# Out-projection of a hybrid decoder layer: token tiles 1 to 6 formed in three pairs, by seven half products a pair instead of eight

## What is computed

```
y = jnp.concatenate([ya, yb, yc, yd.astype(x.dtype)], axis=-1) @ w_out[l]
x = x + gt1 * y
h2 = rms_norm(x, norm2_g[l]) * (1.0 + sc2) + sh2
x = x + gt2 * hier_moe(h2, moe_w_grp[l], moe_b_grp[l], moe_w_exp[l], moe_b_exp[l],
                       moe_w_gate[l], moe_w_up[l], moe_w_down[l])
```

## Time and profile before

| | |
|---|---|
| time, median of 3 runs | 858.77 us (858.05 to 859.92) |
| the profiled execution, its own time | 855.52 us |
| its span | 853.8 us |
| TensorE busy | 800.3 us, 94% of the span |
| VectorE busy | 467.6 us, 55% |
| chain that ended last | TensorE 76%, VectorE 13%, issue 3%, DMA 3% |
| mean granted TensorE clock | 0.983 of full |
| moved by DMA | 136.30 MB, mean 160 GB/s |

### The profile page before, as it was taken

One profiled execution on the slowest core, in us unless ns is written; L12 is line 12 of the kernel. 1 busy time (PEld: TensorE's weight loads), 2 busy tenths in 40 slices (PEclk: granted clock), 3 DMA queues, 4 the chain that ended last, 5 costly groups with the idle time before them and its releaser, 6 DMA issues.

```text
span 853.8 us, 16617 instructions
## 1 busy us (share of the span) xinstructions
PE 800.3 (94%) x6791; PEld 534.1 (63%) x6791; DVE 467.6 (55%) x1174; ACT 236.2 (28%) x565; POOL 283.7 (33%) x267
## 2 busy tenths in 40 slices
PE   8999999999999999798989999999899999999950
PEld 8557544454444444787776555555888888888830
DVE  3850468888742134889873344354745555554534
ACT  6320021111200031466542122212232223232214
POOL 5820000000299800744660000000235656543332
PEclk9999999999999999999999999999999999999995
DMA  9934433344201020300003851213889999988639
GB/s 319 334 94 136 148 123 124 123 149 157 90 25 50 25 74 16 136 4 4 5 5 147 317 203 50 87 63 123 323 316 302 305 273 278 275 266 261 209 66 385
DMA packets 79716, 136.30 MB, mean 160 GB/s; under 512 B 17213, under 2 KB 51226, under 8 KB 79642
## 3 DMA queue, kind: packets, MB, share of 16 engines
q1 hardware_dynamic: 69338, 118.44, 39.9%
q0 software_dynamic: 10304, 16.82, 8.4%
HBM read 124.18 MB, written 29.92 MB: 180 GB/s over the span
## 4 chain that ended last, share of the span: by engine, by line
PE 76%; DVE 13%; issue 3%; DMA 3%; ACT 2%; POOL 1%; SPq 1%; DVEq 0%; POOLq 0%; ACTq 0%
PE banks L791 71%; PE banks L1430 3%; DVE REG_Y L1790 3%; DVE REG_P L2392 1%; DVE REG_P L2041 1%; POOL REG_P L677 1%; PE banks L1361 1%; ACT REG_P L1478 1%; DMA REG_P<-y_d 1%; ACT REG_W L1478 1%; DMA prow<-in_conv_w 1%; DVE REG_W L1897 1%; DVE REG_P L1790 1%; DVE mx L1900 1%; DMA y_d<-REG_Y,idx 1%
## 5 line engine op out<-in xcount | busy, mean ns | idle before, releaser
L791 PE MATMUL banks<-REG_W 128*128 128x512 f32 (+2 forms) x832 | 273.0, 497 | 0.3 <-DVE REG_W L1830 0.3
L791 PEld LDWEIGHTS banks<-REG_W 128*128 128x128 f32 (+1 forms) x832 | 125.6, 182 | 133.1 <-issue 132.3
L791 PE MATMUL banks<-REG_W,REG_Y 128*128 128x512 f32 x256 | 118.3, 600 | 1.4 <-DVE REG_Y L2347 1.1
L1478 ACT ACTIVATE REG_P<-banks 128x256 f32<-128x256 f32 (+2 forms) x102 | 46.4, 480 | 144.8 <-PE banks L791 126.4
L791 PE MATMUL banks<-REG_P 64*64 64x64 f32 (+3 forms) x2496 | 72.4, 236 | 11.3 <-issue 4.5
L791 PEld LDWEIGHTS banks<-REG_P 64*64 64x64 f32 (+1 forms) x2496 | 62.4, 138 | 20.4 <-issue 9.1
L1478 ACT ACTIVATE REG_Y<-banks,mod,s 128x128 f32<-128x128 f32 x136 | 51.1, 456 | 86.0 <-PE banks L1430 86.0
L791 PEld LDWEIGHTS banks<-REG_W,REG_Y 128*128 128x128 f32 x256 | 45.6, 191 | 44.3 <-issue 44.1
L791 PEld LDWEIGHTS banks<-REG_Y,REG_P 128*128 128x128 f32 (+1 forms) x616 | 63.1, 181 | 6.7 <-issue 6.7
L791 PE MATMUL banks<-REG_Y,REG_P 128*128 128x128 f32 (+1 forms) x616 | 66.5, 276 | 0.0
L635 POOL TENSOR_TENSOR REG_P<-REG_P 128x1040 f32<-128x1040 f32 x2 | 4.8, 2386 | 175.8 <-DVE REG_P L1876 175.8
(11 more groups left out here) (297 smaller groups left out, 1107.7 us busy)
## 6 DMA issues: line engine op xcount, KB each, us to landing
REG_P<-in_w_ada SPq DMA_DIRECT2D x20, 1024.0 KB, 6.7
REG_W<-in_w_in SPq DMA_DIRECT2D x17, 512.0 KB
REG_P<-in_moe_w_gate SPq DMA_DIRECT2D x17, 512.0 KB, 8.5
REG_W<-in_moe_w_gate SPq DMA_DIRECT2D x16, 512.0 KB, 5.7
REG_W<-in_moe_w_up SPq DMA_DIRECT2D x16, 512.0 KB, 10.1
REG_W<-in_moe_w_down SPq DMA_DIRECT2D x16, 512.0 KB, 16.3
REG_P<-in_moe_w_up SPq DMA_DIRECT2D x14, 512.0 KB, 14.5
REG_P<-in_moe_w_down SPq DMA_DIRECT2D x12, 512.0 KB, 21.2
```

The costliest lines, as they stand in the source:

```text
L791: return pe.matmul(o_, l, r, start=start, stop=stop, skip_group_check=True)
L1478: return act.activation(o_, i_, f, **kw)
```

## The change

Tiles 0 and 7 keep their 16 matmuls each (tile 7 takes some of them through sums that exist anyway). Tiles 1 to 6 form pairs `i` = 1, 2, 3 of tiles `b` = 2i-1 and `a` = 2i. A product is 4 matmuls of 128x512 (4 blocks `k`, one half `h`); a pair now has 7 products, 28 matmuls instead of 32. For that, VectorE makes:

- once: weight sums `w3` (two steps of 128x1024), `w2` (one step of 128x2048), the upper-right quarter of the weights overwritten (`columns_replaced`, 128x2048), and `w4` (two steps of 128x1024);
- per pair: four sums of rows (`rows_joined` two, `rows_replaced`, `rows_last`, 128x512 each), and nine additions of 128x512 to form the rows of `x1`, where four stood before; one of the PSUM banks is first copied to `u2` by ScalarE.

`w2`, `w3` and `w4` stand in REG_W where places 0 and 1 of the ring were. The places are numbered anew, and the loads move: experts 0 to 2 are issued early, 3 when tiles 0 to 6 are stored, 4 and 5 at the end of the out-projection, 6 behind the store of tile 7, and 7 to 10 when routing is done.

```diff
+        HK, HN = KD // 2, D // 2
+        w4, o = area(REG_W, (KD - 2) * D, HK, HN)
+        w3, o = area(REG_W, o, HK, HN)
+        w2, o = area(REG_W, o, HK, HN)
+        y1, o = area(REG_S, 0, HK, P)
+        u2, o = area(REG_S, o, HN)
...
-            for e in range(5):
+            for e in range(3):
                 load_expert(e, TURN[e], s_w[e])
...
             sp.wait_ge(s["st_x1"], 16 * (NT - 1))
+            load_expert(3, TURN[3], s_w[3])
+            sp.wait_ge(s["op_ps"], 2)
+            load_expert(4, TURN[4], s_w[4])
             load_expert(5, TURN[5], s_w[5])
-            sp.wait_ge(s["op_ps"], NT)
+            store_tile(NT - 1)
             load_expert(6, TURN[6], s_w[6])
-            load_expert(7, TURN[7], s_w[7])
-            store_tile(NT - 1)
-            load_expert(8, TURN[8], s_w[8])
...
-            for e in range(9, RING):
+            for e in range(7, RING):
                 load_expert(e, TURN[e], s_w[e])
...
+            product(1, 1, lower)
+            x1_turned(0)
+            product(1, 1, upper)
+            product(1, 7, lower)
+            logits(0)
+            product(1, 7, upper)
+            product(1, 2)
+            ranks(0)
+            product(1, 5)
+            listed(0)
+            product(1, 6)
+            product(1, 4)
+            product(1, 3, lower)
+            x1_turned(1)
+            product(1, 3, upper)
+            for i in range(2, PAIRS + 1):
+                b, a = 2 * i - 3, 2 * i - 2
...
+                product(i, 5)
+                product(i, 6)
+                ranks(a)
+                product(i, 4)
+                product(i, 3, lower)
+                x1_turned(a + 1)
+                product(i, 3, upper)
...
+            columns_joined()
+            rows_joined(1)
+            dve.wait_ge(s["xr_ld"], 16 * (NT - 1))
+            summed_rows(0)
+            turned_rows(0)
+            columns_replaced()
+            choices(0)
+            rows_replaced(1)
+            columns_last()
+            seventh(1)
+            second(1)
+            rows_last(1)
+            entered_lists(0)
...
+            for i in range(2, PAIRS + 1):
+                b, a = 2 * i - 3, 2 * i - 2
+                choices(b)
+                turned_rows(a)
+                rows_replaced(i)
+                seventh(i)
+                entered_lists(b)
+                second(i)
+                rows_last(i)
+                choices(a)
+                fifth(i)
+                if i < PAIRS:
+                    rows_joined(i + 1)
+                else:
+                    rows_of_last_tile()
+                sixth(i)
+                entered_lists(a)
+                fourth(i)
+                turned_rows(a + 1)
+                third(i)
+            choices(NT - 3)
+            turned_rows(NT - 2)
+            entered_lists(NT - 3)
+            choices(NT - 2)
+            entered_lists(NT - 2)
+            summed_rows(NT - 1)
```

More of the change, by code:

```diff
@@ new lines, in out_last @@
+            def out_last(q, ks=range(KD // 2)):
+                at = slice((NT - 1) * P, NT * P)
+                if ks[0] == 0:
+                    if q == 0:
+                        pe.wait_ge(s["att_y_then_op_u"], NT + 4 * PAIRS)
+                    elif q == 1:
+                        pe.wait_ge(s["op_x1"], NT - 2)
+                    elif q == 3:
+                        pe.wait_ge(s["att_nm_then_op_y"], NT + 4 * PAIRS + 1)
+                for k in ks:
+                    rows = (yT[:, k, at], yT[:, k, at], yT[:, 4 + k, at], y1[:, k])[q]
+                    cols = (wo_at(k, 0), w3[:, k], wo_at(4 + k, 0), wo_at(4 + k, 1))[q]
+                    last = mm(PS[2 + q % 2][:, :], rows, cols, k == 0 and q < 2, k == KD // 2 - 1 and q >= 2)
+                if q == 3 and k == KD // 2 - 1:
@@ L1364, in logits @@
             def logits(j):
+                pe.wait_ge(s["rt_hot"], j)
                 for k in range(KD):
@@ L1390, in _ @@
             pe.wait_ge(s["w_y"], 2 * TURNS)
-            out_main(0, range(0, 1))
+            out_first(range(0, 1))
             norm_sums(tail_norm(TURNS - 1), sqt, tail_squares(TURNS - 1))
-            out_main(0, range(1, 4))
+            out_first(range(1, 4))
             norm_flip(tail_norm(TURNS - 1))
-            out_main(0, range(4, 5))
+            out_first(range(4, 5))
             norm_back(tail_norm(TURNS - 1))
[L1397 to L1411, removed]
+            out_first(range(5, KD))
@@ new lines, in _ @@
+            lower, upper = range(0, 2), range(2, 4)
+            product(1, 1, lower)
[15 more added lines that the diff above has]
+                b, a = 2 * i - 3, 2 * i - 2
+                product(i, 1, lower)
+                logits(b)
+                product(i, 1, upper)
+                x1_turned(a)
+                product(i, 7, lower)
+                if i > 2:
+                    listed(b - 1)
+                product(i, 7, upper)
+                ranks(b)
+                product(i, 2, range(0, 3))
+                listed(b)
+                logits(a)
+                product(i, 2, range(3, 4))
+                product(i, 5)
[5 more added lines that the diff above has]
+                product(i, 3, upper)
@@ L1412, in _ @@
+            out_last(0, lower)
+            logits(NT - 3)
+            out_last(0, upper)
+            x1_turned(NT - 2)
+            out_last(1, lower)
+            listed(NT - 4)
+            ranks(NT - 3)
+            out_last(1, upper)
+            out_last(2, lower)
+            listed(NT - 3)
+            logits(NT - 2)
+            out_last(2, upper)
+            out_last(3)
+            ranks(NT - 2)
             beside(4, 0)
@@ L2218, in modulated, with columns_joined @@
                 last.then_inc(s[done], 1)
+            def columns_joined():
+                dve.wait_ge(s["wo_sc"], 2 * KD)
+                dve.wait_ge(s["w_y"], 2 * TURNS)
+                for n in range(2):
+                    ks = slice(2 * n, 2 * n + 2)
+                    ch.note(tt(w3[:, ks], wo_a[:, ks, HN:], (wo_a[:, 4:6, HN:], wo_b[:, :, HN:])[n], ALU.subtract))
+                ch.wait()
+                dve.sem_inc(s["att_pn_then_op_w"], 1)
+                tt(w2, wo_a[:, 0:HK, 0:HN], w3, ALU.subtract).then_inc(s["att_pn_then_op_w"], 1)
@@ L2220, in summed_rows, with third @@
+            def third(i):
+                dve.wait_ge(s["att_qk_then_op_p"], 2 * NT + 7 * i)
+                a = corner(2 * i, 1)
+                tt(a, PS[1][:, :], a, ALU.add).then_inc(s["op_x1"], 1)
             def summed_rows(j):
-                dve.wait_ge(s["op_ps"], j + 1)
+                dve.wait_ge(s["op_ps"], 1 if j == 0 else 2)
                 if j == NT - 1:
```

168 lines of the change are left out of this document (134 added, 34 removed).

## The result

The changed kernel takes 866.61 us (median of 6 runs, 863.94 to 869.41), the kernel before 858.41 us (6 runs, 856.57 to 859.92). The ratio is 1.0094, interval 1.0072 to 1.0117: slower by 8.2 us, forecast +9.3. The profiled execution took 868.59 us, with a granted clock of 0.971 over its span, where it was 0.983.

A forecast was written before the change was run, and what follows sets the result against it. The prediction took TensorE and weight delivery as limits ending together. Out-projection savings were eaten by waits and clock (shift 0); two experts +9.6, lead -0.3, gave +9.3: 858.8 to 868 us, range 859 to 872.5.

The forecast's parts named there:

- The products: Out-projection: three products of 3.43 us each go, taking 10.3 us from TensorE.
- The waits for VectorE: Out-projection: TensorE waits 3.6 for tile 0's sum, 2.8 for its lists, 1.3 at pairs' transposes, 1.1 at the end; 8.8 us.
- The clock: Out-projection: half clock behind the two new waits loses 1.5 us; bounds nothing, or 3.4 for two.
- its bounds: End of routing: done as late as before, shift 0, bounds -2.5 to +2.5 us.
- The two experts: Behind the routing: two more experts to deliver, 4.8 us each, +9.6; 3.8 undisturbed as lower end, 5.05 at 90.2% of engine time.
- from there goes at the pace of the weights, about 8.1 us an expert: Expert stretch: after first waiting at expert 25 or 26, TensorE is held to the weights' delivery.
- Rivals 2 and 3: Out-projection: VectorE not in the way, 857.8 us, chance 0.12; deliveries: no limit, 857.3 or 858.8 us, chance 0.07.
- worse case: Last six experts: waits bring 1.2 GHz clock, or an expert costs up to 8.3; 872 to 880 us, chance 0.11.
- VectorE isn't in the way: Out-projection: waits of 8.8 and clock of 1.5 don't come, routing ends 10.3 earlier; 857.8 us, chance 0.12.
- delivery isn't a limit: Expert stretch: the 0.3 us lead at expert 31 is chance, time follows routing; 857.3 or 858.8 us, chance 0.07.
- two limits end at the same moment: Expert 31: TensorE and weight delivery both limit; taking work from TensorE alone gains nothing beyond 0.3 us.
- The rule weighed: Expert stretch: queues share the same 16 DMA engines, so weights can't overtake gathers and two experts cost the full 9.6 us.

The follow-up runs named there:

- experiment 4: Changed kernel with tile 0's sum first, its lists one product later, and tile 7's sum ahead of tile 6's lists: 857.28 us, ratio 0.9976.
- Experiment 6: Changed kernel with all three waits for VectorE reordered away and experts 9 and 10 loading only 16 of 1024 columns: 852.36 us, ratio 0.9904.
- experiment 2: Changed kernel with experts 9 and 10 loading only 16 of 1024 columns of each array: 860.43 us, ratio to before 1.0001.
- experiment 3: Changed kernel with VectorE's sum of tile 0 moved ahead of the weight sum `w2` and the sums of rows: 862.14 us, ratio to before 1.0034.
- experiment 1: Kernel before with only the new places and order of the weight loads, all arithmetic as before: 866.20 us, ratio 1.0071.
- 5: Kernel before with experts 9 and 10 loading only 16 of 1024 columns of each array: 858.68 us, ratio 0.9987.
- experiment 8: Reordered kernel with gate and up of expert 3 and gate of 8 loaded early, 7 and rest of 8 behind the first gathers: 860.53 us, ratio 1.0002.
- experiment 7: Reordered kernel with gate and up of expert 3 and gate of 8 early, 7 and rest of 8 behind tile 7's store: 856.84 us, ratio 0.9966.
- experiment 9: Reordered kernel with experiment 8's early arrays plus gate and up of expert 6, up and down of 7, in the weight sums' space: 856.87 us, ratio 0.9963.

## Why the prediction was right, and where it was off

**The products.** -10.3 us: three products of 3.43 us. From the end of tile 0 to the loads that the end of the out-projection releases it was 120.2 us before (476.49 to 596.68). In experiments 4 and 6 it is 111.7 each (478.66 to 590.38, 479.85 to 591.58), at full clock throughout and with 0.8 us of waits in it: 9.3 us saved. Experiment 6, with shares of other waits in it, gives -8.2 by its time.

**The waits for VectorE.** Forecast 3.6, 2.8, 1.3 and 1.1, together 8.8; measured 3.3, 2.4, 0.7 and 1.5, together 7.9. All four stand where the order on VectorE said. The prices from the earlier trace rows held: 2.29 us for 2048 elements (2.4 taken), 1.22 for 1024 (1.25).

**The clock.** +1.5 was too low; the profile loses 3.0 us behind the first wait, near the upper bound of 3.4, and nothing behind the second. What one wait costs isn't fixed, though: behind the same wait of 3.3 us experiment 2 has 3.4 us of half clock instead of 6.8, and behind the same wait of 2.4 us experiment 3 has some and the changed kernel none. With 9.3 for the products the sum is +1.6, and the routing ends 1.4 later in the trace instead of 0, within its bounds. Experiment 2 shows about the same in the times: 1.0001.

**The two experts.** The mechanism is shown: 1 puts the loss in the loads alone, and 2 takes it away with the bytes. The term of +9.6 us was mis-sized. TensorE lost 4.5 us in waits and 1.6 by the clock, 6.1, and experiment 1 measures the same 6.1. From the release to expert 31's last landing it was 195.2 us against 189.9: the two experts lengthen the whole stretch by only 5.3 us, 2.65 each, under the lower bound of 3.8. But up to expert 24 it was 147.4 against 133.9: 13.5 us, 6.7 each, above the 5.05 that bounded my term. I had taken one price for the whole stretch, and it is neither. The time that the weights hold the engines was nearly right. In the whole stretch, first before and then after:

```profile
q1 hardware_dynamic: 10548, 37.91, 57.1%
q1 hardware_dynamic: 11415, 41.07, 59.8%
```

57.1% of 189.9 us are 108.5, 59.8% of 195.2 are 116.7: 8.2 more, 4.1 an expert where I had 4.8. What I had wrong was that all of it lengthens the stretch: 5.3 did, queue 0 held the engines 1.4 us less, and the rest went into time in which they had been free.

**The step that failed** is "from there goes at the pace of the weights, about 8.1 us an expert". The first waits came at 25 and 26 as forecast, but then the gathers had run out, and an expert took 6.5 us of queue, little over TensorE's 6.17. Expert 31 landed at 818.6 (forecast 817, but in a profile that ran 4.2 us late at tile 0; without them it is 814.4). That the sum came out as close as it did is in part luck: the products and the clock were together 2.5 us too good, VectorE's waits 0.9 and the deliveries 3.2 us too dear, and these errors cancel in part. The profile gives 1.4 + 6.1 = 7.5, the medians 8.2, the forecast was 9.3. The missing 0.7 between profile and medians are within the scatter; I don't assign them.

**The chances.** Rivals 2 and 3 have 0.19 together and both end at "faster" or "same", yet these two got only 0.17, and "slower" 0.83 where forecast and worse case have 0.81. It changes nothing here, but the two lists should agree.

**Rivals.** That VectorE isn't in the way falls with the waits and with 3 and 4. That delivery isn't a limit is true of the kernel before (5) and false of the changed one (1, 2): "two limits end at the same moment" fits these runs, and it meant that the time hung on neither the bytes alone nor, for more than the lead, on TensorE alone. The worse case had half of its mechanism: the clock did fall behind a wait for weights, but once, for 1.6 us.

**The rule weighed** (Trainium skill, *DMA: Bandwidth & Descriptors*, section *Issuing engines are not separate DMA queues*): the queues share the engines. The traces agree: as the share of queue 0 went from 32.5 to 20.1%, that of queue 1 rose from 55.0 to 70.3%. What I had drawn from it, that the two experts cost their full 9.6 us, doesn't follow: they cost 6.1.

## What to carry to other kernels

Scratch space for a trick on the arithmetic is paid with what stood there: if it was prefetch, work out the lead of every later transfer over its use, before and after, and where it crosses zero. A lead that ends at 0.3 us is no measure of slack, and the loss from crossing it is what the engine then waits, not the transfers' whole cost, and here it ended when the gathers did. With the new additions in, look at what the critical engine's next step waits for and put that first: here two moved steps on VectorE were worth about 5 us, in a change whose whole gain is 8.

## What the runs showed of the hardware

- The same 1.573 MB cost 3.8 us at the undisturbed rate, 6.7 us in the busy middle of the expert stretch, 2.65 us over its whole length, and nothing that can be measured in the kernel before.
- In or right behind waits of 3.3, 2.9 and 5.3 us began stretches at half clock of 3.4 to 6.8 us. TensorE was still waiting in a part of some, so they cost 1.7 to 3.0 us each. Behind one of 2.2 us in experiment 8 there was such a stretch too, while behind those of 2.4 and 1.7 us in experiment 4 there was none; and behind the same wait of 3.3 us it was 6.8 us in one kernel and 3.4 in another (experiment 2). A wait's own length is thus no measure of its price.
- Arrays issued before the first gather seem to hold TensorE up in two ways: 1.8 us of wait became 5.3 in experiment 7, where the gather itself took 7.6 us instead of 4.9 with the DMA engines at 1.02 and 387 GB/s, and 4.2 in experiment 9, where the store that the gather waits for took 10.5 us instead of 8.1. Each was seen in one profile.
- Stretches at half clock come also at places without any change (0 to 40 and 380 to 400 us), in one profile and not in the other. Runs of one kernel differ by up to 8 us, and the mean granted clock of each run goes with it: in experiment 9 the five fastest (854.8 to 856.3 us) have 0.978 to 0.981, the two slowest (862.6 and 863.0) 0.969 and 0.971. So these stretches are a good part of the scatter; what brings them on isn't known.
